# Modulation weights on VectorE instead of TensorE, in a float32 model block on one core

## The reference

```python
s_lat = jax.nn.silu(c)
s_ctx = jax.nn.silu(c_ctx)
for layer in range(DEPTH_2):
    shift, scale, gate = jnp.split((s_lat @ ada_w[layer] + ada_b[layer])[:, None, :], 3, axis=-1)
    h = rms_norm(x, pre_g[layer]) * (1.0 + scale) + shift
    shift_c, scale_c, gate_c = jnp.split(s_ctx @ ada_w[layer] + ada_b[layer], 3)
    hc = rms_norm(ctx, pre_g[layer]) * (1.0 + scale_c) + shift_c
    ...
    x = x + gate * rms_norm(y, post_g[layer])
```

## Time and profile before

| | |
|---|---|
| median of 3 runs | 3446.28 us (3445.81 to 3447.62) |
| the profiled execution | 3447.18 us, span 3445.3 us |
| granted TensorE clock, mean | 0.985 |
| TensorE, VectorE, ScalarE busy | 96%, 45%, 42% of the span |
| read from memory | 551.60 MB, 161 GB/s over the span |

### The profile page before, as it was taken

The page is one execution under the profiler, slowest core; times in us unless marked ns, Lnnn a source line. Parts: engine busy times, 40 slices in busy tenths (PEclk is TensorE's granted clock), DMA queues, the critical chain, the costliest instruction groups (busy, mean ns, idle before and its releaser), DMA issues.

```text
span 3445.3 us, 48626 instructions
## 1 busy us (share of the span) xinstructions
PE 3302.9 (96%) x20886; PEld 2867.6 (83%) x20886; DVE 1547.3 (45%) x2033; ACT 1431.2 (42%) x1986; POOL 32.7 (1%) x30
## 2 busy tenths in 40 slices
PE   7999999899999999999999999999799999999998
PEld 7989998698999987767777778778689888888886
DVE  4444545455555554446332322242444444454554
ACT  5444544544444444446322222232554345444453
POOL 0000002000000000000000000000000000000000
PEclk9999999999999999999999999999999999999999
DMA  6665544655665666666455555432222333332333
GB/s 205 183 190 175 153 147 159 229 186 212 212 234 206 240 219 241 235 229 219 147 162 173 171 159 174 162 129 98 92 81 92 98 105 100 97 108 89 105 131 120
DMA packets 349062, 557.00 MB, mean 162 GB/s; under 512 B 16880, under 2 KB 148976, under 8 KB 347696
## 3 DMA queue, kind: packets, MB, share of 16 engines
q1 hardware_dynamic: 346304, 540.08, 47.5%
q0 software_dynamic: 2256, 13.11, 1.0%
q10 hardware_dynamic: 288, 0.70, 0.1%
HBM read 551.60 MB, written 2.23 MB: 161 GB/s over the span
## 4 chain that ended last, share of the span: by engine, by line
PE 53%; ACT 5%; DVE 4%; issue 2%; DMA 1%; DVEq 0%; ACTq 0%
PE ps L622 47%; PE ps L641 2%; ACT whi L986 2%; PE ps L806 1%; PE ps L828 1%; ACT hA L1154 1%; PE ps L810 1%; DVE hA L1711 1%; PE ps L824 1%; ACT L1154 1%; DVE wlo L1486 1%; PE ps L669 1%; DVE hA L1703 1%; DMA raw<-in_w_ple_gate 0%; DVE hB L1700 0%
## 5 line engine op out<-in xcount | busy, mean ns | idle before, releaser
L1486 DVE TENSOR_TENSOR wlo<-raw,whi 128x1024 fp32r<-128x1024 f32 x819 | 1001.2, 1230 | 1500.5 <-ACT whi L986 1492.5
L986 ACT ACTIVATE whi<-raw 128x1024 fp32r<-128x1024 f32 x824 | 861.3, 1057 | 1351.0 <-PE ps L622 669.4
L622 PE MATMUL ps<-HCh,whi 128*128 128x512 f32 (+1 forms) x1664 | 605.8, 364 | 0.9 <-DVE HCl L1550 0.9
L622 PE MATMUL ps<-HCl,whi 128*128 128x512 f32 (+1 forms) x1664 | 595.0, 358 | 0.0
L622 PE MATMUL ps<-HCh,wlo 128*128 128x512 f32 (+1 forms) x1664 | 594.9, 358 | 0.0
L622 PE MATMUL ps<-Vh,whi 128*128 128x256 f32 x1408 | 404.9, 288 | 14.5 <-DVE wlo L1486 14.4
L622 PE MATMUL ps<-Vh,wlo 128*128 128x256 f32 x1408 | 399.5, 284 | 0.0
L622 PE MATMUL ps<-Vl,whi 128*128 128x256 f32 x1408 | 399.3, 284 | 0.0
L622 PE MATMUL ps<-whi,HCh 128*128 128x256 f32 (+1 forms) x1152 | 378.2, 328 | 4.5 <-DVE M L1500 4.5
L622 PEld LDWEIGHTS ps<-HCh,whi 128*128 128x128 f32 x1664 | 316.1, 190 | 65.7 <-issue 17.8
L622 PE MATMUL ps<-whi,HCl 128*128 128x256 f32 (+1 forms) x1152 | 369.0, 320 | 0.0
(11 more groups left out here) (298 smaller groups left out, 4124.9 us busy)
## 6 DMA issues: line engine op xcount, KB each, us to landing
raw<-in_ada_w SPq DMA_DIRECT2D x192, 512.0 KB, 6.8
raw<-in_w_up SPq DMA_DIRECT2D x176, 512.0 KB, 4.7
raw<-in_w_in SPq DMA_DIRECT2D x160, 512.0 KB, 3.7
raw<-in_od_w_in SPq DMA_DIRECT2D x160, 512.0 KB, 3.5
raw<-in_ev_w_in SPq DMA_DIRECT2D x96, 512.0 KB, 6.3
raw<-in_w_down SPq DMA_DIRECT2D x88, 512.0 KB, 4.9
raw<-in_w_out SPq DMA_DIRECT2D x32, 512.0 KB, 5.0
raw<-in_w_ple_gate SPq DMA_DIRECT2D x32, 512.0 KB, 4.7
```

What stands on the lines that cost most here:

```text
L622: mm = e.matmul(o, a, b, start=first and t == 0, stop=last, skip_group_check=True)
L986: e.activation(m.whi[ch.i % SPLIT][:, 0:n], m.raw[ch.slot][:, 0:n], ACT.Copy).then_inc(S("hi"), 1)
L1486: e.tensor_tensor(m.wlo[ch.i % SPLIT][:, 0:n], m.raw[ch.slot][:, 0:n], m.whi[ch.i % SPLIT][:, 0:n].bitcast(F32), ALU.subtract).then_inc(S( ...
```

## The change

1. The chunks of `ada_w` come one at a time ("units", eight to a group). VectorE multiplies the chunk's values by the vector's value of each partition and adds them up in `ACC` (128 x 512 for each vector), 4 instructions of 128x512 for a chunk: `tensor_scalar` at the first row block of a group, `scalar_tensor_tensor` at the others. For the last four groups only one vector is needed (2 instructions). VectorE releases the raw buffer.
2. TensorE only adds `ACC` up over the partitions at a group's end: 8 (or 4) products with one column of ones. It waits for VectorE's last instruction of the group. Transposes, the copy to `R` and the additions of parts go.
3. The units stand elsewhere: 32 behind chunks of the input projection, 64 behind those of `out`, `up` and `down`, 96 behind those of `pg` and the even layer. The pairs that stood in a bunch are gone.
4. `root`'s dummy square root is issued earlier (`warm`), ahead of the copies and sums of the group before the norm.
5. SBUF is laid out anew (`G` in the place of `lb`, `hgm` in that of `cw`, loaded later; `z`, `e` and `ji` share `ACC`'s place), TensorE waits for the first four groups before the attention, and the memsets of two PSUM banks go.

```diff
-ADA1 = 0.165
-ADA2 = 0.47
+ADA_EARLY = 32
...
+def ada_vectors(g):
+
+    l, m = ADA_GROUPS[g]
+    return (0,) if l == 1 and m >= 8 else (0, 1)
...
+            u = Unit()
+            u.g, u.j = divmod(self.units, 8)
...
+            u.ch = self.chunk(self.W_ada[l][u.j * 256:(u.j + 1) * 256, m * 512:(m + 1) * 512].rearrange(
+                "(k p) c -> p k c", p=128), 2, 512, False, True)
...
+    p.limit = ADA_EARLY
     for g in range(12):
+        p.rate = ADA_EARLY / 84 if g else 0.0
         p.group(f"in{g}", A["w_in"], g * 512, 512, NT, T, tm=g in (6, 7, 8, 11))
...
+    p.limit, p.rate, p.due = 96, (96 - ADA_EARLY) / 274, 0.0
...
+    p.limit, p.rate, p.due = 192, 0.4, 0.0
+    for g in range(4):
+        p.group(f"pg{g}", A["w_ple_gate"], g * 512, 512, NT, T, tm=True,
+                quiet=(range(8), (), (), range(4, 8))[g])
+    p.rate = (192 - p.units) / 91
...
 def sync(m, e):
...
             old = plan.chunks[ch.c - RING]
-            if old.i is None:
-                e.wait_ge(S("mm"), old.c + 1)
+            if old.end is not None:
+                e.wait_ge(S("ada"), old.end)
+            elif old.i is None:
+                e.wait_ge(S("mm"), old.n)
             else:
                 e.wait_ge(S("lo_" + old.lane), old.n_lo)
...
 class Tensor(Engine):
...
+        if u.j < 7:
+            return
+        e.wait_ge(S("ada"), u.ch.end)
+        if u.g > 1:
+            e.wait_ge(S("ada_M"), u.g - 1)
+        for v in u.vs:
+            for i in range(4):
+                t = e.matmul(m.PS[6 + u.g % 2][:, 4 * v + i:4 * v + i + 1], m.ACC[:, v, 128 * i:128 * i + 128],
+                             m.ones[:, 0:1], start=True, stop=True, skip_group_check=True)
+        t.then_inc(S("ada_sum"), 1)
...
 class Scalar(Engine):
...
+    def warm(self):
+
+        self.e.activation(self.m.SM[:, 24:25], self.m.ones[:, 0:1], ACT.Sqrt)
...
 class Vector(Engine):
...
+        if u.j == 0 and u.g:
+            e.wait_ge(S("ada_sum"), u.g)
+        e.wait_ge(S(f"raw{u.ch.slot}"), u.ch.landed)
+        W = m.raw[u.ch.slot][:, :].rearrange("p (k c) -> p k c", k=2)
+        n = u.before
+        for k in range(2):
+            for v in u.vs:
+                x = 2 * (2 * u.j + k) + v
+                acc, s = m.ACC[:, v, :], m.Sv[:, x:x + 1]
+                if u.j == k == 0:
+                    t = e.tensor_scalar(acc, W[:, k, :], s, None, ALU.mult)
+                else:
+                    e.wait_ge(S("ada"), n + 1 - len(u.vs))
+                    t = e.scalar_tensor_tensor(acc, W[:, k, :], s, acc, ALU.mult, ALU.add)
+                t.then_inc(S("ada"), 1)
+                n += 1
```

## The result

The changed kernel takes 3969.4 us (median of 4 runs, 3964.5 to 3971.0) against 3447.0 for the kernel before on the same chip: ratio 1.151, 95% interval 1.149 to 1.153. I had predicted 3828 us with a range of 3710 to 3950. The direction and the mechanism were right, the time is 141 us above the forecast and outside the range. The profiled execution has a span of 3968.7 us. Executions of one kernel differ by some us (13 of the kernel before lie between 3442.4 and 3450.8), so a difference of a few us between kernels that ran once is not certain.

What follows compares the result with a forecast made beforehand. TensorE, busy 96%, was taken to bound the kernel before; afterwards a loop through VectorE and the five-buffer ring. Even layer 201 + projection 121 + out to down 52 + gate 18 - rest 10 = +382 us: 3828 us, range 3710 to 3950.

Steps and rivals of the forecast that it cites:

- the mechanism: All stretches with units: a buffer's refill waits for VectorE's unit, putting landing and split on VectorE's path; chance 0.80.
- Rival A: Whole kernel: TensorE stays the bound, the ring hides everything, 2.5 us waits at 24 eighth units; 3397 us, chance 0.06.
- B: Rival: the loop closes in the even layer alone, other work covers the landing elsewhere; +127, 3574 us, chance 0.06.
- The projection: Input projection: cycles of 10.0, 11.4 and 12.7 us make 353 us for 82 chunks that took 231.5; +121 us.
- Gate: Gate of the per-layer embedding: 78 us for 17 chunks that took some 50, less 8 pairs; +18 us.
- the group's eighth unit: In out, up, down: TensorE waits for it, then does sums and three chunks; 2.2 us late, 8 groups, 18 us.
- the burst's fourth transfer: In out, up, down: the fourth transfer after a unit's end lands 7.65 us after it.
- out to down: Stretches out, up and down: cycles 66, evacuations 42, group ends 18, less removed work and waits; +52 us.
- the removed work: In out, up, down, taken off: 48 pairs 56 us, 11 turns 4 us, low-half waits 14 us.
- the evacuations: In up: 22 evacuations of 3.4 us on VectorE cost 0 to 4 us each, taken as 2; 42 us.
- Even layer: 8.9 us per product (7.6 with one vector), 752 us for 91 chunks that took 550.8; +201 us.
- rival C: Even layer: TensorE's clock falls to 1.2 GHz and it is the bound again; +218 more, 4046 us, chance 0.08.

Runs made afterwards that it cites:

- e1: Changed kernel with VectorE's units placed in the ring's order, right behind the low half of the product before: 3362.9 us, ratio to before 0.976.
- e2: Changed kernel without TensorE's column sums; VectorE adds the bias to columns of ACC instead: 3845.8 us.
- e13: Changed kernel with 44 filler products of 128x128 on TensorE before each wait of the column sums: 3937.7 us.
- e9: e1 with each group's eighth unit (and none of the next group before it) back at its own place on VectorE: 3444.0 us, ratio to before 0.999.
- e10: e1 with one column sum per group in place of eight (four in the last four groups): 3331.4 us, ratio to before 0.966.
- e8: Changed kernel with two instead of eight instructions in each of the 22 evacuations of up: 3932.2 us.
- e12: Changed kernel with only the first half of each chunk of w_up transferred: 3944.6 us.

## Why the prediction was wrong, point by point

**The mechanism held.** e1 shows that the order of units and low halves on the one ring costs all of the loss and hides a gain. Rivals A and B fall: every stretch with units is longer, and TensorE rests in each. The turn of the even layer was worked out within 3% (8.9, measured 8.65 to 8.8). The projection without its group ends is 127 us longer (e2), against 121. Gate 24 against 18, rest -8 against -10, table 4.6 against 5.

**The step that failed: the group's eighth unit.** I had TensorE wait until that unit ends (E), then do the sums and three split chunks at full clock until E + 9.9. The high half of the burst's fourth transfer, which needs the buffer that these free, was then 2.2 us late, 8 times: 18 us in out to down. In every other stretch I put the ends at nothing. Without the ends 123 us go (e2): 61 in out to down and 62 elsewhere. The runs show what I had wrong.

*The backlog runs at the low clock.* The rows are an end in `up`: the unit on VectorE and the first and third high half behind it on ScalarE. The third belongs to the burst's fourth transfer, since one of the transfers is a modulation chunk. First the changed kernel, then e13 at the same place, where the clock is 1.00:

```profile
1158.45 2.73 DVE L1513 SCALAR_TENSOR_TENSOR ACC<-raw,S,ACC 128x512 f32<-128x512 f32 x4
1169.48 1.06 ACT L984 ACTIVATE whi<-raw 128x1024 fp32r<-128x1024 f32 x1 [12.58 <-PE ps L640]
...
1175.13 1.06 ACT L984 ACTIVATE whi<-raw 128x1024 fp32r<-128x1024 f32 x1 [1.76 <-PE ps L640]
```
```profile
1147.60 2.74 DVE L1516 SCALAR_TENSOR_TENSOR ACC<-raw,S,ACC 128x512 f32<-128x512 f32 x4
1155.37 1.06 ACT L987 ACTIVATE whi<-raw 128x1024 fp32r<-128x1024 f32 x1 [9.32 <-PE ps L640]
...
1161.02 1.06 ACT L987 ACTIVATE whi<-raw 128x1024 fp32r<-128x1024 f32 x1 [1.77 <-PE ps L640]
```

Each waits for TensorE. In e13 the third starts 10.7 us after the unit's end, close to my 9.9. In the changed kernel it is 14.0 (8.3 for the first in place of 5.0), so the low clock adds 3.3 us, where I had counted it as filling idle time. Against a landing of 8.4 us the high half is some 5.5 us late, not 2.2.

*The end of a looped stretch.* Behind the last end of the projection and of the even layer TensorE is the bound again, and its whole backlog counts: 12 and 17 of the 123 us. I had no term for it. Of the other 10 and 10 us in these two stretches e13 gives back 8 and 11, so they too are mostly the clock.

e9 gives the price without the loop: 3.4 us of wait and 6.2 us in all for 13 ends, half wait, half clock. Rival A had the length of the wait about right (2.5 us; ten of the 13 are 2.3 to 2.7) and left out the clock. Without the ends the forecast would have been 3810 and e2 is 3846, well inside its range.

**Out to down, the rest of it.** Without ends it is +101 us, and I had 34. Of these 67 us: the removed work gave less (e10, which has hardly any sums, is 62 us under before; I had 74), 12; the evacuations 47 instead of 42 (e8), 5; the fourth transfer of a burst lands 8.4 (up) to 8.7 us (out, down) after the request instead of 7.65, 43 us over 51 turns, of which e12 lets 0.45 per us count, about 20. Some 30 us stay open. The parts of 12 and 5 us are near the 8 us by which executions of one kernel differ, so this split is an estimate.

**Even layer, overpriced.** +155 without its ends, against 201. The turn is 0.1 to 0.25 us shorter than I had (6 to 14 us over 56 units). And TensorE takes the products up to the stretch's first sums in 46 us (2027.3 to 2073.5), at its own pace of 5.5 us for most of them, on what was split ahead, where I had counted eight turns of 8.9 (71): about 25 less. Some 10 us are left over. I had used the steady state from the first unit.

**The clock.** The granted clock fell as rival C says, to 0.50 in front of all 24 sums, and e13 prices the long stretches at 32 us, at most some 68, not 218. I had argued that a slow chunk fills its own idle time. That holds between the ends: e2 has none and is still at the low clock for 382 us (before: 108), with 254 of these 274 us more in dips shorter than 10 us, and lies within 36 us of the forecast, which had no term for the clock. It does not hold behind an end, where ScalarE waits for the slow backlog. The page "TensorE: Matmul & The Clock Gate" of the Trainium skill (Why this matters for your kernels) says that an idle array pays again at each burst. This trace agrees for the clock, 0.50 after each long wait. What it costs depends on who is the bound: 36 us for 74 us of low clock where it is TensorE (e9), 32 to 68 us for 281 where it is the loop.

**The range.** It was made of landing, unit length and evacuations, each varied alone. The term that failed had a point value and no bounds.

## What to carry to other kernels

When work moves from a waiting engine to one that also feeds a shared ring, take each release in the ring's order: look whether the engine frees a buffer just before it needs that buffer's next content. Give such work the same lead, in microseconds, as the other users of the ring. And where an engine meets another only every eighth time, bound that meeting by the whole lead it can have gained, and price the backlog behind it at the clock that the rows show after such a wait. Count the backlog once more where the slow loop ends.

## What the runs showed of the hardware

- A column sum (128x128 float32 stationary, one moving column) costs TensorE 0.23 us in the stream at full clock (40.6 us for 176); 152 of them less gave 31 us, 0.21 each.
- 281 us less at the low clock gave 32 us where VectorE was the bound, with fillers some 36 us longer than the waits they filled (e13). Where TensorE was the bound, 74 us more came with 36 us more of busy time for the same products (e9).
- A burst of 512 KB transfers lands mostly in steps of 1.3 to 1.6 us. In the turn in `down1` the first two stand 3.3 us apart (1621.6 and 1624.9), and there the second request took 1.5 us to issue instead of 0.5.
